# Two attentions of one Trainium2 kernel: where VectorE's copies of transposed rows and the late query tiles stand in the engines' order

## The chip, the cores and the metric

One core of one Trainium2 chip runs one program. The metric is device time in microseconds of one execution; the median of several executions is given. Five engines work beside each other, each through its own list of instructions in order: TensorE (matmuls and transposes, PE in the profile; its weight loads are PEld), VectorE (DVE), ScalarE (ACT), GpSimd (POOL) and SyncE (SP, which issues DMAs). They meet at counting semaphores. All data here is 32-bit.

## The reference, cut to what matters

For 512 tokens of width 1024 a first block (windowed attention, gated convolution, 32 routed experts) is followed by two attention layers, each with an MLP. The two attentions behind the experts are the ones that the change touches:

- layer 0: eight heads of a forgetting attention ("fox": causal softmax with a bias from a running sum) and eight heads of a latent attention over the 256 keys with the best index scores:

```
logits = einsum('bqhd,bshd->bhqs', qb, k) * scale + cq - cum_k     # fox
p = masked_softmax(logits, causal);  o = einsum('bhqs,bshd->bqhd', p, v)
logits = (qa . c_sel + qr . kr_sel) * scale                        # latent
p = masked_softmax(logits, valid);   o = einsum('bqhk,bqkr->bqhr', p, c_sel)
```

- layer 1: sixteen heads with three gated branches, over compressed keys, over selected blocks and over a window:

```
p_c = masked_softmax(s_c, cmp_end <= t);  p_s = masked_softmax(s_s, ...);  p_w = masked_softmax(s_w, ...)
out = gb0 * o_c + gb1 * o_s + gb2 * o_w
```

## The kernel before, in words

Both attentions are software pipelines over items, with an order per engine that is written out by hand. An item is one head and one tile of 128 queries; with query tile t (0 to 3) it is 128 rows by (t+1)*128 keys wide, so 128, 256, 384 or 512 wide.

**Layer 0** has 64 items (`pairs`): for fox and then latent, for four head pairs, for t = 0 to 3, two heads. So items 8m to 8m+7 are one head pair, and their widths are 128, 128, 256, 256, 384, 384, 512, 512. **Layer 1** has 136 items (`nsa`): eight groups of 17 (t = 0, 1, 2, 3 and then 3, 2, 1, 0), each of 16 items (four heads, two branches, two key groups) and one item of compressed scores ("cmp"), 256 wide.

An item goes through these steps, and each engine's loop over i says at which of its steps item k's turn comes:

1. TensorE: scores of item i into a PSUM bank (L1743 and, for fox, L1749; in layer 1 L2389).
2. VectorE: mask and negated maximum of item i in one instruction, from PSUM into one of seven SBUF tiles `scr` (L3935; in layer 1 L4079). Called the maximum below. Before it stands a wait that the tile is free: the transposes of item i-7 have to be done (`wait_ge(p_turned, i - PROBS + 1)`, L3934, and L4069), with PROBS = 7.
3. ScalarE: exponential with row sums (L2433 is the line of its helper).
4. VectorE: reciprocals of two row sums at once (`weigh_pair`, L3923; `weigh_nsa`, L4046, and for a cmp item L4049 to L4052).
5. GpSimd: the product with the reciprocal (L1419; L1443, L1439).
6. TensorE: transposes of item k, at its step i = k + 7, into `psT[k % 2]` (L1765; L2402). There are only these two banks of PSUM for them, so before the transposes of item k it waits until item k-2 has been copied out (`p_copied`, `n_copied`).
7. The copy of the transposed rows into SBUF: even k on ScalarE, odd k on VectorE (L3945; L4087). In VectorE's loop the copy of item k stands at step i = k + 6, behind the maximum of item k + 6 and ahead of that of item k + 7.
8. TensorE: products with the values (L1731; L2352, L2342), at its steps k + 10, once per four items.

In layer 0 TensorE computes the scores of items i and i+1 together at even i. VectorE also takes the low half of finished outputs (L3089, `pair_out_lo`, `nsa_out_lo`), at step k + 13 for the last item k of a head pair.

The waits and the order at the copy in layer 0, on VectorE:

```
if i >= PROBS:
    dve.wait_ge(p_turned, i - PROBS + 1)
nc.vector.tensor_tensor_reduce(out=pair_probs[i % PROBS]..., in0=pair_bank(i)..., accum_out=negm...)
if 2 <= i < n_pairs and i % 2:
    weigh_pair(i)
k = i - TURN_LAG - 1                      # TURN_LAG is 5
dve.wait_ge(p_turned, k + 1); tensor_copy(pair_turned[k % TURNED]..., psT[k % 2]...)
```

**Late query tiles.** In layer 1 four of the eight query tiles (queries 4 to 7) and four sets of compressed scores are made inside the loop, as eight jobs (`NSA_JOBS`) at TensorE's steps `NSA_STEPS`. They use two banks in turn, so a job waits until the job two before it has been taken out. A query tile is taken out by two copies on ScalarE (`queries`, the high parts) and then two subtractions on VectorE (L3089, `nsa_q`). TensorE has filler matmuls that compute nothing needed (L2360) at steps 4 to 15. For i < 16 the scores of layer 1 have two banks, so the scores of item i wait for the maximum of item i-2; later there are four.

The constants at the head of the file: `TURN_LAG, VALUE_LAG = 5, 8`, `PROBS, TURNED = 7, 8`, `AHEAD, MORE_BANKS = 2, 16`.

Of the kernel before, what the change touches and what calls it, by code (L numbers as in the profile page):

```python
# [39 lines left out]
TURN_LAG, VALUE_LAG = 5, 8  # L40
# [114 lines left out]


NSA_JOBS = (("cmp", 0), ("cmp", 1), ("query", 4), ("query", 5), ("query", 6), ("query", 7), ("cmp", 2), ("cmp", 3))
NSA_STEPS = (3, 4, 5, 6, 7, 9, 12, 13)


def nsa_job(what, n):
# [213 lines left out]
def build(nc, w, out):  # L375
    ctx = ExitStack()
    with ctx:
# [307 lines left out]
        for g in range(2):  # L685
            for t in range(NT):
                lo, hi = max(0, t - 1), min(NT - 1, t + 1)
                n = (hi - lo + 1) * P
# [1734 lines left out]
        def _(act):  # L2423
# [11 lines left out]
            def evac(n, o, width=512, f=ACT.Copy, **kw):  # L2435

                product(act, n)
                A(o, bank(n)[:, 0:width], f, **kw).then_inc(proj_evacuated[n % 2], 1)
# [582 lines left out]
            def queries(j):  # L3021

                if j < 4:
                    act.wait_ge(nsa_turned, j + 1)
                    o = early_bank(j)
                else:
                    product(act, nsa_job("query", j))
                    o = bank(nsa_job("query", j))
                A(query(j, 0)[0:HD, :], o[0:HD, :], ACT.Copy)
                A(query(j, 1)[HD:P, :], o[HD:P, :], ACT.Copy).then_inc(stack_hi, 1)  # L3030

            def nsa_attention():

                for i in range(n_nsa + VALUE_LAG + AHEAD + 2):
                    if i in PRESPLIT:
                        if i == PRESPLIT[0]:
                            act.wait_ge(n_scores, n_nsa // 2)
                        first_weights("no0", PRESPLIT.index(i))
                    if i - 1 in NSA_STEPS:
                        what, n = NSA_JOBS[NSA_STEPS.index(i - 1)]  # L3040
                        if what == "query":
                            queries(n)
                        else:
                            evac(nsa_job("cmp", n), cmp_scores[:, n, :])
                    k = i - TURN_LAG - 1
                    if 0 <= k < n_nsa and k % 2 == 0:
                        act.wait_ge(n_turned, k + 1)
                        if k >= TURNED:
                            act.wait_ge(n_values, values_before(k - TURNED))
                        A(turned_probs[k % TURNED][:, 0:nsa[k]["n"]], psT[k % 2][:, 0:nsa[k]["n"]], ACT.Copy)\  # L3050
                            .then_inc(n_copied[k % 2], 1)
                    if i < n_nsa:
                        act.wait_ge(n_masked, i + 1)
                        at = probs[i % PROBS][:, 0:nsa[i]["n"]]
                        if nsa[i]["kind"] == "cmp":
                            A(at, at, ACT.Exp).then_inc(n_probs, 1)
                        else:
                            A(at, at, ACT.Exp, bias=negm[:, n_items + i:n_items + i + 1], scale=-1.0,
                              accum_out=sums[:, n_items + i:n_items + i + 1]).then_inc(n_probs, 1)
                    k = i - VALUE_LAG - AHEAD - 1  # L3060
                    if k in bank_ending:
                        it = nsa[k]
                        act.wait_ge(n_values, values_before(k))
                        A(nsa_out_hi[it["c"]][:, :, it["t"] * P:(it["t"] + 1) * P],
                          psO[it["bank"] % 2][:, :].rearrange("p (j n) -> p j n", j=4), ACT.Copy).then_inc(n_out_hi, 1)
# [13 lines left out]
        def _(dve):  # L3079
# [845 lines left out]
            def pair_attention():  # L3925

                for i in range(n_pairs + VALUE_LAG + AHEAD + 4):
                    if i == n_pairs + 1:
                        weigh_pair(i)
                    if i < n_pairs:  # L3930
                        it, col = pairs[i], n_band + i
                        dve.wait_ge(p_scores, i + 1)
                        if i >= PROBS:
                            dve.wait_ge(p_turned, i - PROBS + 1)  # L3934
                        nc.vector.tensor_tensor_reduce(  # L3935
                            out=pair_probs[i % PROBS][:, 0:it["n"]], in0=pair_bank(i)[:, 0:it["n"]], in1=it["mask"], scale=-1.0,
                            scalar=3e38, op0=ALU.add, op1=ALU.min, accum_out=negm[:, col:col + 1]).then_inc(p_masked, 1)
                    if 2 <= i < n_pairs and i % 2:
                        weigh_pair(i)
                    k = i - TURN_LAG - 1  # L3940
                    if 0 <= k < n_pairs and k % 2:
                        dve.wait_ge(p_turned, k + 1)
                        if k >= TURNED:
                            dve.wait_ge(p_values, batches_before(k - TURNED))
                        nc.vector.tensor_copy(pair_turned[k % TURNED][:, 0:pairs[k]["n"]], psT[k % 2][:, 0:pairs[k]["n"]])\  # L3945
                            .then_inc(p_copied[k % 2], 1)
                    k = i - VALUE_LAG - AHEAD - 3
                    if 0 <= k < n_pairs and k % 8 == 7:
                        chunk = pairs[k]["chunk"]
                        dve.wait_ge(p_out_hi, k // 8 + 1)  # L3950
                        tt(pair_out_lo[:, chunk, :], psO[pairs[k]["bank"] % 2][:, :], hT_hi[:, chunk, :].bitcast(F32), ALU.subtract)\
                            .then_inc(p_out_lo, 1)
# [105 lines left out]
            def nsa_attention():  # L4058

                for i in range(n_nsa + VALUE_LAG + AHEAD + 4):  # L4060
                    if i == 1:
                        compressed_values()
                    elif i - 2 in NSA_STEPS and NSA_JOBS[NSA_STEPS.index(i - 2)][0] == "query":
                        queries(NSA_JOBS[NSA_STEPS.index(i - 2)][1])
                    if i < n_nsa:
                        it = nsa[i]
                        dve.wait_ge(n_scores, i + 1)
                        if i >= PROBS:
                            dve.wait_ge(n_turned, i - PROBS + 1)  # L4069
                        at = probs[i % PROBS][:, 0:it["n"]]  # L4070
                        if it["kind"] == "cmp":
                            s3 = at.rearrange("p (j n) -> p j n", j=8)
                            st = cmpst[:, it["index"], :]
                            link(tt(s3, score_bank(i)[:, 0:256].rearrange("p (j n) -> p j n", j=8),
                                    cmpmask[:, it["t"], :].unsqueeze(1).broadcast_to([P, 8, 32]), ALU.add))
                            link(nc.vector.tensor_reduce(st, s3, X, ALU.max))
                            tt(s3, s3, st.unsqueeze(2).broadcast_to([P, 8, 32]), ALU.subtract).then_inc(n_masked, 1)
                        else:
                            nc.vector.tensor_tensor_reduce(  # L4079
                                out=at, in0=score_bank(i)[:, 0:it["n"]], in1=cmask(it["t"]), scale=-1.0, scalar=3e38,  # L4080
                                op0=ALU.add, op1=ALU.min, accum_out=negm[:, n_items + i:n_items + i + 1]).then_inc(n_masked, 1)
                    k = i - TURN_LAG - 1
                    if 0 <= k < n_nsa and k % 2:
                        dve.wait_ge(n_turned, k + 1)
                        if k >= TURNED:
                            dve.wait_ge(n_values, values_before(k - TURNED))
                        nc.vector.tensor_copy(turned_probs[k % TURNED][:, 0:nsa[k]["n"]], psT[k % 2][:, 0:nsa[k]["n"]])\  # L4087
                            .then_inc(n_copied[k % 2], 1)
                    if 2 <= i < n_nsa + 2 and nsa[i - 2]["g"]:
                        weigh_nsa(i - 2)  # L4090
                    k = i - VALUE_LAG - AHEAD - 3
                    if k in bank_ending:
                        it = nsa[k]
                        span = (slice(None), slice(None), slice(it["t"] * P, (it["t"] + 1) * P))
                        dve.wait_ge(n_out_hi, it["bank"] + 1)
                        tt(nsa_out_lo[it["c"]][span], psO[it["bank"] % 2][:, :].rearrange("p (j n) -> p j n", j=4),
                           nsa_out_hi[it["c"]][span].bitcast(F32), ALU.subtract).then_inc(n_out_lo, 1)
# [34 lines left out]
```

## Time and profile before

| what | value |
|---|---|
| median of 3 runs | 1916.68 us (1914.93 to 1918.02) |
| the profiled execution's own time | 1919.38 us |
| its span in the trace | 1917.6 us |
| busy, share of the span | PE 96%, PEld 76%, DVE 54%, ACT 43%, POOL 31% |
| chain that ended last | PE 86%, DVE 4%, DMA 4%, ACT 3%, issue 2% |
| layer 0's pipeline in the trace | about 808.5 to 887 us |
| layer 1's pipeline in the trace | about 1375 to 1540 us |

The profile shows one execution. Times are microseconds from the span's start. A row of the timeline has start, duration, engine, line, operation, what it writes and reads, how many instructions were merged and, in brackets, how long the engine stood idle before it and what ended that. The duration of a matmul row contains the time until its result is there; the next row can start before it is over.

### The profile page before, as it was taken

The numbers are of one execution on the slowest core, as the hardware profiler recorded it, in microseconds if no ns is written. First come the engines' busy times: TensorE is split into PE (matmuls) and PEld (weight loads), VectorE is DVE, ScalarE is ACT, GpSimd is POOL, SyncE is SP. The second block draws the span as 40 slices with busy tenths as digits, with TensorE's granted clock in tenths as the row PEclk, the third lists the DMA queues.
The fourth block names the chain that finished last, engine by engine and source line by source line (L and its number), as shares of the span: only waits on it lengthen the run. The fifth ranks groups of instructions, "written<-read, shape, count | busy, mean of one in ns | idle before, by whom it ended". The sixth has DMA issues, their size and how long they took to land.

```text
span 1917.6 us, 27389 instructions
## 1 busy us (share of the span) xinstructions
PE 1839.3 (96%) x10554; PEld 1451.5 (76%) x10554; DVE 1027.5 (54%) x2006; ACT 828.2 (43%) x1569; POOL 592.6 (31%) x421
## 2 busy tenths in 40 slices
PE   8999999997888999999999999999999999999998
PEld 7878889842223778767888888889888888888886
DVE  3170442521111869663477676842577725767677
ACT  4123651311111543375554544353377655444543
POOL 4344431011110233356322223233055643232221
PEclk9999999999999999999999999999999999999999
DMA  7223404699999412121132223222203012233321
GB/s 236 98 94 118 140 1 154 251 392 419 420 420 370 167 45 88 46 88 35 54 132 88 88 88 120 98 94 67 45 2 89 2 44 88 88 131 108 113 88 45
DMA packets 86867, 252.06 MB, mean 131 GB/s; under 512 B 12212, under 2 KB 19700, under 8 KB 74448
## 3 DMA queue, kind: packets, MB, share of 16 engines
q1 hardware_dynamic: 81344, 238.79, 33.9%
q0 software_dynamic: 4592, 9.30, 1.3%
q8 instruction: 86, 1.41, 0.3%
q10 hardware_dynamic: 800, 2.20, 0.3%
q14 instruction: 45, 0.37, 0.1%
HBM read 241.89 MB, written 15.73 MB: 134 GB/s over the span
## 4 chain that ended last, share of the span: by engine, by line
PE 86%; DVE 4%; DMA 4%; ACT 3%; issue 2%; POOL 0%; ACTq 0%; DVEq 0%; POOLq 0%
PE psA L1606 42%; PE psS L2054 4%; PE psA L1649 3%; DMA ring<-in_w_down_e 3%; PE psA L2018 2%; PE psO L2352 2%; PE psO L1836 2%; PE psT L1836 2%; PE psS L1836 2%; PE psT L2402 2%; DVE x L3089 2%; DMA big<-in_w_down_e 1%; PE psA L1471 1%; PE psA L1785 1%; PE psS L1649 1%
## 5 line engine op out<-in xcount | busy, mean ns | idle before, releaser
L1290 POOL TENSOR_TENSOR w_slot<-ring,w_slot 128x1024 fp32r<-128x1024 f32 (+1 forms) x81 | 214.0, 2656 | 524.7 <-ACT w_slot L2433 524.4
L1606 PE MATMUL psA<-hT_hi,w_slot 128*128 128x512 f32 x960 | 298.2, 390 | 0.0
L2433 ACT ACTIVATE w_slot<-ring 128x1024 fp32r<-128x1024 f32 (+2 forms) x183 | 196.8, 1086 | 164.4 <-DVE ring L3089 75.0
L1606 PEld LDWEIGHTS psA<-hT_hi,w_slot 128*128 128x128 f32 x960 | 180.4, 188 | 37.3
L1606 PE MATMUL psA<-hT_lo,w_slot 128*128 128x512 f32 x480 | 187.0, 390 | 0.0
L3089 DVE TENSOR_TENSOR w_slot<-ring,w_slot 128x1024 fp32r<-128x1024 f32 x98 | 119.9, 1225 | 115.7 <-ACT w_slot L2433 115.7
L3089 DVE TENSOR_TENSOR x<-psA,x 128x512 f32<-128x512 f32 (+1 forms) x186 | 117.1, 662 | 104.2 <-PE psA L1606 68.8
L1606 PE MATMUL psA<-w_slot,hid_part 128*128 128x512 f32 x672 | 161.4, 390 | 0.0
L2433 ACT ACTIVATE big<-psA 128x512 f32<-128x512 f32 (+6 forms) x134 | 61.7, 482 | 208.7 <-PE psA L1606 126.0
L1606 PEld LDWEIGHTS psA<-w_slot,hid_part 128*128 128x128 f32 x672 | 126.2, 188 | 26.1
L2433 ACT ACTIVATE scr<-scr,stat 128x384 f32<-128x384 f32 (+3 forms) x224 | 123.7, 555 | 19.1 <-DVE stat L4079 9.8
L1290 POOL TENSOR_TENSOR ring_lo<-ring,early_hi 128x1024 fp32r<-128x1024 f32 x34 | 82.6, 2432 | 123.1 <-ACT early_hi L2433 123.1
L1443 POOL TENSOR_SCALAR scr<-scr,stat,big 128x128 f32<-128x128 f32 (+3 forms) x128 | 77.5, 616 | 98.0 <-DVE stat L4046 97.8
L1606 PEld LDWEIGHTS psA<-hT_lo,w_slot 128*128 128x128 f32 x480 | 90.2, 188 | 18.5
L2433 ACT ACTIVATE hid_part<-scr 128x512 fp32r<-128x512 f32 x98 | 59.7, 625 | 98.3 <-DVE scr L3089 98.3
L3089 DVE TENSOR_TENSOR hid_part<-scr,hid_part 128x512 fp32r<-128x512 f32 x98 | 99.1, 1035 | 3.0 <-ACT hid_part L2433 1.8
L2054 PE MATMUL psS<-ring,big 128*64 128x512 f32 x192 | 75.9, 686 | 19.9 <-issue 19.9
L3089 DVE TENSOR_TENSOR big<-psA,small 128x512 f32<-128x512 f32 x32 | 20.6, 685 | 135.1 <-PE psA L1471 135.1
L2433 ACT ACTIVATE big<-psS 128x256 f32<-128x256 f32 (+3 forms) x26 | 8.4, 338 | 187.0 <-PE psS L2054 162.0
L1606 PE MATMUL psA<-hT_lo_early,early_hi 128*128 128x512 f32 x224 | 88.2, 394 | 0.0
L1606 PE MATMUL psA<-w_slot,hT_hi 128*128 128x256 f32 x384 | 71.5, 289 | 1.3 <-DVE big L1147 1.1
L2433 ACT ACTIVATE big<-psT 128x384 f32<-128x384 f32 (+3 forms) x120 | 50.8, 424 | 49.8 <-PE psT L2402 31.3
(557 smaller groups left out, 4450.2 us busy)
## 6 DMA issues: line engine op xcount, KB each, us to landing
ring<-in_mlp_w SPq DMA_DIRECT2D x32, 2048.0 KB, 8.1
ring<-in_w_in SPq DMA_DIRECT2D x8, 2048.0 KB, 8.1
ring<-in_w_gate_e SPq DMA_DIRECT2D x14, 1024.0 KB, 16.3
ring<-in_w_up_e SPq DMA_DIRECT2D x14, 1024.0 KB, 20.7
ring<-in_w_down_e SPq DMA_DIRECT2D x13, 1024.0 KB, 28.3
big<-in_w_down_e SPq DMA_DIRECT2D x12, 1024.0 KB, 26.4
ring<-in_ab_w_in SPq DMA_DIRECT2D x5, 2048.0 KB, 8.6
scr<-in_w_down_e SPq DMA_DIRECT2D x7, 1024.0 KB, 27.0
```

Source lines behind the costliest of these rows:

```text
L1290: nc.gpsimd.tensor_tensor(part(w_lo, c), raw_piece(c), part(w_hi, c).bitcast(F32), ALU.subtract)\
L1443: nc.gpsimd.tensor_scalar(at, at, fac[:, n_items + i:n_items + i + 1], gate3[:, it["t"], it["head"], 1 + it["branch"]:2 + it["branch"]], A ...
L1471: ins = pe.transpose(o[:, c * P:c * P + k], a, ident[0:k, 0:k])
L1606: ins = pe.matmul(o, a, b, start=(at == 1), stop=(at == 3 * len(terms)))
L1649: return pe.matmul(o[:, :], a[:, t * P:(t + 1) * P], b[:, k, :], start=(not h and at == 0), stop=(h == 1 and at == 3 * HALF - 1))
L1836: ins = pe.matmul(KEPT_BANK[q][t][:, :], a[:, k, at], b[:, k, :], start=(not e and k == 0 and a is hi and b is wh), stop=(e == LAST - 1 an ...
L2018: ins = pe.matmul(o[at:at + ROWS, :], ehidT[:, p, k * P + at:k * P + at + ROWS], dn[(2 * b + half) % UNITS][:, k, part * 512:(part + 1) * ...
L2054: ins = pe.matmul(psS[p][at:at + ROWS, :].rearrange("p (h n) -> p h n", h=2), xT[:, p, k, at:at + ROWS], gu[(2 * b + half) % UNITS][:, k], ...
L2352: ins = pe.matmul(o[HD * g:HD * (g + 1), at:at + P], v2[:, b, branch, g, 0:HD], pt[g][:, b * P:(b + 1) * P], start=(it["first"] and not br ...
L2402: ins = pe.transpose(psT[k % 2][:, b * P:(b + 1) * P], probs[k % PROBS][:, b * P:(b + 1) * P], ident)
L2433: return nc.scalar.activation(o, i, f, **kw)
L3089: return nc.vector.tensor_tensor(o, a, b, op)
```

## The change

Three places, in both attentions:

- VectorE's copy of odd item k moves from step k + 6 to step k + 8 in layer 0 and from step k + 6 to step k + 7 in layer 1. In layer 1 `weigh_nsa` is moved ahead of the copy within a step.
- In layer 1, ScalarE takes a late query tile out at TensorE's step of that tile instead of one step later, ahead of its own copy and exponential of that step; VectorE at one step later instead of two.
- Query 6 is made at TensorE's step 8 instead of 7.

```
-NSA_STEPS = (3, 4, 5, 6, 7, 9, 12, 13)
+NSA_STEPS = (3, 4, 5, 6, 8, 9, 12, 13)
...
-                    if i - 1 in NSA_STEPS:
-                        what, n = NSA_JOBS[NSA_STEPS.index(i - 1)]
-                        if what == "query":
-                            queries(n)
-                        else:
-                            evac(nsa_job("cmp", n), cmp_scores[:, n, :])
+                    if i in NSA_STEPS and NSA_JOBS[NSA_STEPS.index(i)][0] == "query":
+                        queries(NSA_JOBS[NSA_STEPS.index(i)][1])
+                    if i - 1 in NSA_STEPS and NSA_JOBS[NSA_STEPS.index(i - 1)][0] == "cmp":
+                        n = NSA_JOBS[NSA_STEPS.index(i - 1)][1]
+                        evac(nsa_job("cmp", n), cmp_scores[:, n, :])
...
@@ VectorE, pair_attention (layer 0)
                     if 2 <= i < n_pairs and i % 2:
                         weigh_pair(i)
-                    k = i - TURN_LAG - 1
+                    k = i - TURN_LAG - 3
                     if 0 <= k < n_pairs and k % 2:
                         dve.wait_ge(p_turned, k + 1)
...
@@ VectorE, nsa_attention (layer 1)
-                    elif i - 2 in NSA_STEPS and NSA_JOBS[NSA_STEPS.index(i - 2)][0] == "query":
-                        queries(NSA_JOBS[NSA_STEPS.index(i - 2)][1])
+                    elif i - 1 in NSA_STEPS and NSA_JOBS[NSA_STEPS.index(i - 1)][0] == "query":
+                        queries(NSA_JOBS[NSA_STEPS.index(i - 1)][1])
...
-                    k = i - TURN_LAG - 1
+                    if 2 <= i < n_nsa + 2 and nsa[i - 2]["g"]:
+                        weigh_nsa(i - 2)
+                    k = i - TURN_LAG - 2
                     if 0 <= k < n_nsa and k % 2:
                         dve.wait_ge(n_turned, k + 1)
                         if k >= TURNED:
                             dve.wait_ge(n_values, values_before(k - TURNED))
                         nc.vector.tensor_copy(turned_probs[k % TURNED]..., psT[k % 2]...)\
                             .then_inc(n_copied[k % 2], 1)
-                    if 2 <= i < n_nsa + 2 and nsa[i - 2]["g"]:
-                        weigh_nsa(i - 2)
```

## Rows read from the trace of the kernel before

**Rows 1.** Layers 0, 1: length, busy PE, PEld, DVE, ACT, POOL, clock, DMA

```profile
808.50:876.00 67.50, 66.05 (x554) 43.52 (x555) 44.21 (x188) 52.85 (x163) 39.81 (x64) 1.00 0.26 95
...
1396.00:1527.00 131.00, 130.10 (x1312) 110.47 (x1304) 101.28 (x396) 98.78 (x309) 80.35 (x125) 1.00 0.13 34
```

**Rows 2.** Waits in 840 to 875: us in total, times, longest

```profile
PEld psT L1765 <- POOL scr L1419: 5.0, 11, 0.5
PE psT L1765 <- DVE big L3945: 1.4, 4, 0.3
```

**Rows 3.** Timeline, layer 0, fox, around the copy of item 15

```profile
831.60 0.69 DVE L3945 COPY big<-psT 128x512 f32<-128x512 f32 x1 [1.22 <-PE psT L1765]
...
832.21 0.68 DVE L3935 CUSTOM_DVE_ANT_0 scr<-psA,const 128x512 f32<-128x512 f32 x1
...
832.43 0.54 PE L1765 MATMUL psT<-const,scr 128*128 128x128 f32 x3
...
833.50 0.27 DVE L3945 COPY big<-psT 128x128 f32<-128x128 f32 x1
```

**Rows 4.** Timeline, layer 0, latent: items 27, 29 and 31

```profile
845.51 0.42 DVE L3945 COPY big<-psT 128x256 f32<-128x256 f32 x1 [1.04 <-PE psT L1765]
...
846.57 0.98 PE L1765 MATMUL psT<-const,scr 128*128 128x128 f32 x7
...
847.16 0.56 DVE L3945 COPY big<-psT 128x384 f32<-128x384 f32 x1 [0.47 <-PE psT L1765]
...
847.63 0.55 DVE L3935 CUSTOM_DVE_ANT_0 scr<-psS,big 128x384 f32<-128x384 f32 x1
...
848.71 0.55 DVE L3935 CUSTOM_DVE_ANT_0 scr<-psS,big 128x384 f32<-128x384 f32 x1
...
849.35 0.77 PE L1765 MATMUL psT<-const,scr 128*128 128x128 f32 x5
...
850.88 0.53 PE L1765 MATMUL psT<-const,scr 128*128 128x128 f32 x3 [0.34 <-DVE big L3945]
```

**Rows 5.** Timeline, layer 1: late query tiles 4 to 7, fillers

```profile
1381.81 1.18 ACT L2433 ACTIVATE nsa_q<-psA 64x512 fp32r<-64x512 f32 x2
...
1383.01 1.39 DVE L3089 TENSOR_TENSOR nsa_q<-psA,nsa_q 64x512 fp32r<-64x512 f32 x2 [0.44 <-ACT nsa_q L2433]
...
1384.46 0.66 PE L1471 MATMUL psA<-const,tok 128*128 128x128 f32 x4 [1.63 <-DVE nsa_q L3089]
...
1388.68 0.66 PE L1471 MATMUL psA<-const,tok 128*128 128x128 f32 x4 [1.86 <-DVE nsa_q L3089]
...
1389.48 0.71 PE L2360 MATMUL psO<-const 128*128 128x160 f32 x4
...
1390.41 1.28 PE L2360 MATMUL psO<-const 128*128 128x160 f32 x4
```

**Rows 6.** Timeline, layer 1: items 25, 59 and 63

```profile
1412.72 0.43 DVE L4087 COPY big<-psT 128x256 f32<-128x256 f32 x1
...
1413.38 0.38 PE L2402 MATMUL psT<-const,scr 128*128 128x128 f32 x2
...
1451.83 0.69 DVE L4087 COPY big<-psT 128x512 f32<-128x512 f32 x1
...
1452.76 0.60 PE L2402 MATMUL psT<-const,scr 128*128 128x128 f32 x4
...
1457.28 0.69 DVE L4087 COPY big<-psT 128x512 f32<-128x512 f32 x1
...
1457.89 0.41 DVE L4049 TENSOR_REDUCE big<-scr 128x8 f32<-128x256 f32 x1
...
1458.46 0.60 PE L2402 MATMUL psT<-const,scr 128*128 128x128 f32 x4
...
1458.72 0.68 DVE L4079 CUSTOM_DVE_ANT_0 scr<-psA,const 128x512 f32<-128x512 f32 x1
```

**Rows 7.** Waits in 1385 to 1535: us in total, times, longest

```profile
PEld psT L2402 <- POOL scr L1443: 2.1, 9, 0.3
```

## The prediction, made before the changed kernel ran

> **What bounds the kernel now.** I read the busy times by stretch first, then the chain, the waits of both stretches and the timeline around VectorE's copies. In both attentions TensorE is as good as full: 66.05 of 67.50 us in layer 0 and 130.10 of 131.00 in layer 1 behind its start, at the full clock, while VectorE is busy for 44.21 and 101.28 [rows 1]. Only the start of layer 1 has real holes: TensorE waits 1.63 and 1.86 us for VectorE to take late query tiles out [rows 5]. So whatever makes TensorE wait inside a pipeline is added to the time nearly whole, and what merely makes VectorE's work earlier gains little. TensorE's list is in order, and its transposes of item k+2 cannot start before item k is copied out of the same bank. The question is therefore how much room there is between the end of a copy and those transposes.
>
> **Layer 0: the copy goes behind two maxima.** Item 15 is the last of a head pair and 512 wide. Its copy starts at 831.60 and ends at 832.29; the transposes of item 17 start at 832.43 [rows 3], 0.14 later, which is what the semaphore takes: no room at all. In the latent half the row says so itself, the transposes waited 0.34 us for the copy [rows 4]. Why does the room vanish there? Between the two transposes TensorE has only items 128 wide to do. Now the copy goes behind the maxima of items k+7 and k+8 and a reciprocal. By the wait in the code the maximum of item k+7 can't start before the transposes of item k are done, which is the very thing that the copy waits for. So the maxima don't fill a hole ahead of the copy; they take its place. From the first of the two maxima to what follows the reciprocal it is 832.21 to 833.50, 1.29 us [rows 3]. The copy is later by 1.29, and so are TensorE's next transposes. There are seven such places (items 7, 15, ... 55; after item 63 no maxima are left): 7 x 1.29 = **9.0 us**.
>
> VectorE starts its next instruction before the last one's recorded end: 1.29 holds two maxima of 0.68 and a reciprocal. The Trainium skill, "VectorE: DVE Perf Modes", section "The DRAIN you can't avoid", says that the next operation does not start until the pipe is empty; if one adds whole durations for that, a delay would be at least 1.36 instead of 1.29 and the seven would give 9.5. The start-to-start times of the rows decide, and by them the recorded ends overlap.
>
> The other odd items have room. In the latent half the 256-wide copy (item 27) ends at 845.93 and the transposes that need it start at 846.57 [rows 4]: 0.50 beyond the 0.14. Two 256-wide maxima and a reciprocal take some 0.76 (an estimate, from the 0.42 of a 256-wide copy with some 0.08 of overlap each): 0.26 too late, four times, 1.0 us. The 384-wide one (item 29) ends at 847.72, its transposes' successors start at 849.35 [rows 4]: 1.49 of room; a maximum and the low half of an output (847.63 to 848.71, 1.08) and a second maximum (0.55) make 1.63: 0.14 too late, four times, 0.5 us. In the fox half TensorE has the bias products in between, and both fit. The 128-wide copies have the value products in between. Layer 0 in sum: 9.0 + 1.0 + 0.5 = **+10.6 us** with the rounding. Bounds: the seven alone at half size (maxima partly done ahead of time, which the wait in the code speaks against), +4.5; all of it, +11.
>
> **Layer 1: the copy goes behind one maximum.** The same two waits stand there. Read item by item, the 67 odd items fall in two halves: for about half the value products stand between the two transposes, and the copy has over 0.6 us of room. For 33 they don't. Item 59: copy from 1451.83, end 1452.52, successors at 1452.76 [rows 6], room 0.10; a 512-wide maximum costs 0.69 with its last part: 0.59 too late. Item 25: copy ends 1413.15, successors at 1413.38 [rows 6], room 0.09; a 384-wide maximum costs 0.55: 0.46 too late. Done so for all 26 places of this kind, they range from 0.2 to 0.6 and give 0.39 in mean: 10.1 us. At seven places, once per group of 17, the copy also falls behind the reciprocals of a cmp item, 1457.89 to 1458.72, 0.83 us [rows 6]: item 63's copy would start about 1458.7 instead of 1457.28, and its successors 1.1 us late; 7 x 1.1 = 7.8. All added, 17.9 us. That is the upper end, since TensorE standing still in one place gives VectorE time to catch up before the next, and where VectorE is behind anyway two such delays aren't paid twice. The lower end is half, 9. I take **+13.5**, the middle: TensorE is full here [rows 1], which argues for the upper end, VectorE is busy 77% of this stretch, which argues for less.
>
> **The start of layer 1: late query tiles earlier.** Query 4 is transposed before 1381. ScalarE takes it out from 1381.81 in 1.18 us, VectorE from 1383.01 in 1.39, and query 6 starts at 1384.46, after 1.63 of waiting; query 7 at 1388.68, after 1.86 [rows 5]. In the changed order ScalarE starts on query 4 a step earlier, about 1380.9, so VectorE is done about 1383.5; and query 6 comes a step later, at about 1384.1. Its wait goes. Query 5 follows on both engines: done about 1385.8, when TensorE has reached query 7. That wait goes too: 3.5 us. What is late next: query 6 is taken out by ScalarE only behind its exponential of item 7, until 1388.0, and by VectorE until 1389.4; behind that stands the maximum of item 9, on which the scores of item 11 wait (two banks). TensorE is there at about 1388.0 and waits until 1389.8. And query 7 holds the maximum of item 10 until 1391.9. Followed on to the transposes of item 5 (step 12), TensorE is there at 1392.4, 2.3 us earlier than now, and I take **-2.0**. Best case: both waits go and so does the stretch at half clock behind them (below), -4.1; worst case 0, if ScalarE's earlier tile makes exponentials late.
>
> **Reciprocals earlier.** In layer 1 they no longer stand behind a copy. GpSimd gets its work earlier, and TensorE's waits for GpSimd are 2.1 us in sum [rows 7]; half of that, **-1.0**; bounds 0 and -2.1. In layer 0 the same row has 5.0 us in 11 waits [rows 2], but they are the weight loads' idle time, while the matmuls waited for VectorE alone 1.4; I give it nothing, at most -1.5.
>
> **Sum.** +10.6 + 13.5 - 2.0 - 1.0 = +21.1 us. The profiled execution took 1919.38 in all (span 1917.6); with the change 1940.5. The median of the runs is 2.7 lower, so the median with the change is **1938 us**.
>
> **Rivals.**
>
> *The copies are harmless, the softmax chain is what counts: faster.* If the maxima, once ahead of the copies, let exponentials, reciprocals and GpSimd run ahead so far that TensorE's transposes stop waiting for GpSimd, and if the room behind a copy is larger than I read, the change gains: 2.0 to 4.1 at the start, up to 2.1 in layer 1 [rows 7] and up to 1.5 in layer 0. About 1911. It decides from the point at which the transposes of item k+2 start less than 0.1 us later than now. Against it stands that they start 0.14 us behind the copy's end now [rows 3], and that the maxima can't start earlier than the transposes allow. Chance 0.12.
>
> *Only layer 0's delays are real.* VectorE in layer 1 is often behind, so one maximum more or less ahead of a copy may vanish in its backlog, and reciprocals come earlier. Then +10.6 - 3.0 and some 2 of layer 1: about 1926. Chance 0.2.
>
> *The waits also cost clock.* After the waits for query tiles TensorE fell from 2.4 to 1.2 GHz for a while: four fillers took 1.28 instead of 0.71 us [rows 5]. A wait of 1.3 us in each head pair is nearly as long as those. If each of the seven brings such a stretch, at about 1.7 us each (an estimate: half of a stretch like that one, in which the scores, transposes and fillers between 1390.2 and 1393.6 took twice their time), it adds up to 12: 1950. The Trainium skill, "TensorE: Matmul & The Clock Gate", section "A second HAM failure mode: psum-queue depth-cycling", describes a kernel whose TensorE idles shortly between groups while it cycles through banks and whose clock swings for it. By that rule this case would come; against it, the 1.63 us wait before query 6 was not followed by it. Chance 0.13.
>
> *Nothing much happens* (delays of one sort make up for gains of the other within 0.2%): chance 0.03, at 1917.
>
> **Numbers.** My own case has 0.52 and about 1931 to 1946. Measurements of this kernel can tell 0.2% from nothing, 3.8 us. Faster 0.12, same 0.04, slower 0.84. The range leaves out the faster case and the farthest of the clock case: 1922 to 1952.
>
> **What would show it.** Right: in the timeline the 512-wide copy of layer 0 starts 1.3 us behind the end of its transposes, after two maxima and a reciprocal; the next transposes carry a wait of 1.3 to 1.5 us for `big` L3945, seven times; a head pair takes 1.3 us longer in fox and 1.7 longer in latent. In layer 1 TensorE waits for `big` L4087 some 30 times for 0.3 to 1.1 us. The queries' transposes at about 1384.1 and 1386 (plus what layer 0 has added) carry no long wait. Wrong: the maxima start ahead of the transposes of item k, the head pair keeps its length, or the gap between the copy's end and the next transposes grows beyond 0.14.

## The result, and the profile after

The changed kernel took 1947.94 us in the median of four runs (1947.32 to 1949.2), the kernel before 1917.35 beside it: ratio 1.0163 [1.0145, 1.018], slower by 31 us. The prediction was 1938, slower by 21. The sign and the mechanism were right and the range of 1922 to 1952 held the time; the sum was 10 us short, and the time lies 2 us above the 1931 to 1946 of the prediction's own case, on the side of the rival with the clock (1950). The profiled execution took 1947.32, its span of 1945.5 is 27.9 longer than before's.

The page's head, and busy times by stretch as in [rows 1] (length, then busy PE, PEld, DVE, ACT, POOL, clock, DMA share, GB/s; the first stretch, 725 to 900, holds the last of the experts' work and layer 0's pipeline, the other two lie inside the pipelines):

```profile
span 1945.5 us, 27389 instructions
...
PE 1843.3 (95%) x10554; PEld 1448.5 (74%) x10554; DVE 1024.6 (53%) x2006; ACT 831.0 (43%) x1569; POOL 592.4 (30%) x421
...
725.00:900.00 175.00, 160.62 (x1079) 122.63 (x1078) 113.85 (x354) 82.04 (x213) 74.83 (x83) 0.98 0.17 61
...
806.00:890.00 84.00, 70.70 (x557) 46.17 (x557) 45.99 (x193) 54.60 (x168) 40.55 (x65) 0.96 0.21 76
...
1407.00:1555.00 148.00, 131.68 (x1301) 108.94 (x1297) 103.04 (x394) 101.13 (x310) 79.72 (x125) 1.00 0.11 30
```

The stretch with the same work before the change:

```profile
727.00:887.00 160.00, 157.28 (x1080) 120.86 (x1080) 113.45 (x353) 82.33 (x213) 75.23 (x84) 1.00 0.19 67
```

Read the rows of 725 to 900 and of 727 to 887 together. The same work (1079 and 1080 matmul entries) took 175 instead of 160 us. TensorE's idle time in it went from 2.7 to 14.4 us, and its busy time from 157.28 to 160.62, at a granted clock of 0.98 instead of 1.00. So layer 0 holds two different losses: 11.7 us of waiting and 3.3 of slower clock. VectorE did the same work, 113.85 and 113.45. In layer 1's pipeline TensorE stands still for 16.3 of 148 us, where it stood for 0.9 of 131 [rows 1]. No engine became the bound; the engines wait in turn.

The waits of layer 0's stretch 805 to 900, then those of 1387 to 1565 (engine, what it wanted to write and its line, what it waited for; us in total, times, longest):

```profile
DVE scr L3934 <- PE psT L1765: 34.3, 27, 4.0
...
PE psT L1765 <- DVE big L3944: 12.8, 15, 1.7
...
PEld psT L1765 <- POOL scr L1419: 1.0, 3, 0.3
```

```profile
DVE scr L4078 <- PE psT L2402: 44.4, 55, 2.8
...
PE psT L2402 <- DVE big L4088: 14.4, 29, 1.2
...
PEld psT L2402 <- POOL scr L1443: 5.7, 8, 1.4
```

For VectorE's copies TensorE waited 1.4 us in 840 to 875 before [rows 2], and not once in layer 1. Now they cost it 12.8 us in layer 0 and 14.4 in layer 1. The first line of each fence is the other half: the maxima (`scr` L3934, L4078) are now what stands first behind a transposition, 27 and 55 times. In layer 0 it was the copies before, and it is one copy now (before in 805 to 890, then the changed kernel in 805 to 900):

```profile
DVE big L3945 <- PE psT L1765: 25.8, 24, 2.6
```

```profile
DVE big L3944 <- PE psT L1765: 3.9, 1, 3.9
```

The maxima did not fill a hole ahead of the copy; they took its place.

Item 15's surroundings in the timeline of the changed kernel (start, duration, engine and line; in brackets how long it waited and for whom), to be laid beside [rows 3]:

```profile
831.62 0.69 DVE L3934 CUSTOM_DVE_ANT_0 scr<-psA,const 128x512 f32<-128x512 f32 x1 [1.22 <-PE psT L1765]
...
832.24 0.69 DVE L3934 CUSTOM_DVE_ANT_0 scr<-psA,const 128x512 f32<-128x512 f32 x1
...
832.85 0.16 DVE L3922 RECIPROCAL stat<-stat 128x2 f32<-128x2 f32 x1
...
832.93 0.67 DVE L3944 COPY big<-psT 128x512 f32<-128x512 f32 x1
...
833.75 0.53 PE L1765 MATMUL psT<-const,scr 128*128 128x128 f32 x3 [1.37 <-DVE big L3944]
```

The maximum starts at 831.62, where the copy stood at 831.60 before. (That the two traces meet here is chance: the changed one came into the layer 1.8 us earlier and had lost as much in the first head pair.) The copy starts at 832.93, 1.31 behind that maximum, and its successors 0.15 behind its end, at 833.75 instead of 832.43. Seven such waits stand in the layer: 1.37 us ahead of items 9 and 17, 1.74 ahead of items 25, 33, 41 and 49 (where 0.34 had been before), and 1.23 ahead of item 57. The same in layer 1, item 63, to be laid beside [rows 6]:

```profile
1475.46 0.41 DVE L4048 TENSOR_REDUCE big<-scr 128x8 f32<-128x256 f32 x1
...
1476.29 0.68 DVE L4078 CUSTOM_DVE_ANT_0 scr<-psA,const 128x512 f32<-128x512 f32 x1
...
1476.90 0.69 DVE L4088 COPY big<-psT 128x512 f32<-128x512 f32 x1
...
1477.73 0.63 PE L2402 MATMUL psT<-const,scr 128*128 128x128 f32 x4 [0.77 <-DVE big L4088]
```

Head pair by head pair (transposes of item 8m+1 to those of item 8m+9, the timeline's start times) layer 0 took, in us:

```
pair         1     2     3      4     5     6      7    sum
before     8.25  9.86  9.82   8.62  8.63  8.64   8.63  62.45
after      9.99 11.20 12.83  10.66 10.57 12.14  10.57  77.96
```

Each pair is 1.3 to 2.0 longer, the latent ones (4 to 7) more than the second and third of fox; two of them, the third and the sixth, carry another 1.6 at half clock.

### The profile page after: what moved, and what is told of

It reads as the page before. It is cut to its first block, busy times and chain, and to the rows that moved or that the text cites. A ratio compares the mean times of both kernels' runs of the same rounds, so it can differ in the third digit from the quotient of the medians.

```text
span 1945.5 us, 27389 instructions
## 1 busy us (share of the span) xinstructions
PE 1843.3 (95%) x10554; PEld 1448.5 (74%) x10554; DVE 1024.6 (53%) x2006; ACT 831.0 (43%) x1569; POOL 592.4 (30%) x421
## 3 DMA queue, kind: packets, MB, share of 16 engines
q8 instruction: 86, 1.41, 0.3%
## 4 chain that ended last, share of the span: by engine, by line
PE 82%; DVE 7%; DMA 5%; issue 3%; ACT 2%; POOL 1%; DVEq 0%; SPq 0%; ACTq 0%; POOLq 0%
PE psA L1606 42%; PE psS L2054 4%; PE psA L1649 3%; DMA ring<-in_w_down_e 3%; PE psA L2018 2%; PE psO L2352 2%; PE psO L1836 2%; PE psT L1836 2%; PE psS L1836 2%; PE psT L2402 2%; DMA big<-in_w_down_e 2%; DVE x L3088 1%; PE psA L1471 1%; PE psA L1785 1%; PE psS L1649 1%
## 5 line engine op out<-in xcount | busy, mean ns | idle before, releaser
L2402 PE MATMUL psT<-const,scr 128*128 128x128 f32 x336 | 60.3, 277 | 16.1 <-DVE big L4088 14.4
```

The costliest lines, as they stand in the source:

```text
L2402: ins = pe.transpose(psT[k % 2][:, b * P:(b + 1) * P], probs[k % PROBS][:, b * P:(b + 1) * P], ident)
```

## The experiments

The theory on record: a copy has as much room as stands between its end and the transposes that reuse its bank; what it is moved beyond that is added whole. The rivals: the lost time comes from the query tiles or the reciprocals; the waits cost clock; room does not matter. Each kernel was timed against the kernel before on the same chip (before's medians 1916.8 to 1917.6); a difference in us is the ratio less 1, times 1917. All compute the whole of the reference.

**e1: only layer 0's copies.**

```
-                    k = i - TURN_LAG - 1
+                    k = i - TURN_LAG - 3
```

> The kernel before with the layer 0 part of the change alone: VectorE's copy two steps later. Theory (the copy is late, and the next transposes wait for it in one of two banks): in the trace of the change layer 0 took 15.6 us more, so +15 to +16 us, some 12.5 us of it waits of the transposes for `big` on VectorE in 15 places and about 3 us from two stretches at 1.2 GHz. Rival (the loss comes from the two parts together, or from the experts ahead, which moved by 1.8 us between the two traces): under +8 us.

Measured: 1931.69, ratio 1.0074 [1.0057, 1.0091], +14.2 us. Its waits in 805 to 900:

```profile
PE psT L1765 <- DVE big L3945: 12.7, 15, 1.7
```

That is the changed kernel's row, almost to the digit. In the trace the layer is 15.5 us longer in both, so layer 0's loss is the copy's alone.

**e2: only layer 1's copies and reciprocals.**

```
-                    k = i - TURN_LAG - 1
+                    if 2 <= i < n_nsa + 2 and nsa[i - 2]["g"]:
+                        weigh_nsa(i - 2)
+                    k = i - TURN_LAG - 2
...
-                    if 2 <= i < n_nsa + 2 and nsa[i - 2]["g"]:
-                        weigh_nsa(i - 2)
```

> The kernel before with the layer 1 order of VectorE alone: reciprocals ahead of the copy, copy one step later; late query tiles as before. Theory: every place where no value products stand between the transposes of items k and k+2 pays one maximum, +18 us by the trace of the change (from item 3 to item 135 the distance between the two traces grew from -2.6 to +15.6 us), less at the start, where the fillers leave room: +17 to +19. Rival (VectorE was behind anyway and the maximum is lost in its backlog): +8 to +12, and the rest of the difference would come from the query tiles.

Measured: 1935.68, 1.0101 [1.0084, 1.0119], +19.4 us, more than the 13.5 - 1.0 of the sum. Its interval, 16.1 to 22.8 us, leaves room for the sum's upper end of 17.9. In the trace it falls back by 18.2 us from item 9 to item 134. Waits in 1384 to 1550:

```profile
PE psT L2402 <- DVE big L4089: 14.4, 29, 1.2
```

e1 and e2 together make +33.6; with e3's -1.3 (below) that is +32.3 against the +31.2 of the whole. The parts add up within their intervals.

**e3: only the query tiles, with query 6 at step 8.** `NSA_STEPS` and both engines' `queries` as in the change, the rest as before.

> The kernel before with the late query tiles alone taken earlier (and query 6 at step 8); both copies where they were. Theory: the transposes of item 5 come 2.6 us earlier, as in the trace of the change, and nothing behind takes it back: -2 to -3 us. Rival (the earlier start runs into the softmax chain of the 128- and 256-wide items, where ScalarE and VectorE are nearly full, and is given back by item 20): 0 to -1.

Measured: 1915.71, 0.9993 [0.9985, 1.0002], -1.3 us. Its late query tiles, beside [rows 5]:

```profile
1381.90 0.65 PE L1471 MATMUL psA<-const,tok 128*128 128x128 f32 x4 [1.14 <-ACT big L2433]
...
1384.01 0.60 PE L1471 MATMUL psA<-const,tok 128*128 128x128 f32 x4
...
1385.30 0.62 PE L1471 MATMUL psA<-const,tok 128*128 128x128 f32 x4
...
1388.96 0.44 PE L2389 MATMUL psS<-nsa_k,nsa_q 128*128 128x128 f32 x2 [1.33 <-DVE stat L4078]
```

Queries 6 and 7 (second and third row) wait no more, as predicted: 3.5 us of waiting gone. In its place stand 1.14 us of query 5 waiting for ScalarE, which the sum did not have, and 1.33 of item 11's scores behind VectorE's maximum of item 9, which it had. Counted from the entry into layer 1, e3 runs 2.5 us ahead of before from item 5 to the end of the layer.

**e4: e3 with the reciprocals ahead of the copies, which keep their step.**

```
+                    if 2 <= i < n_nsa + 2 and nsa[i - 2]["g"]:
+                        weigh_nsa(i - 2)
                     k = i - TURN_LAG - 1
...
-                    if 2 <= i < n_nsa + 2 and nsa[i - 2]["g"]:
-                        weigh_nsa(i - 2)
```

> The same, and the reciprocals of layer 1 ahead of the copy within a step, the copy itself at its old step. Theory: a reciprocal of two columns ahead of the copy costs the copy 0.08 us in half of the places, but once per group of 17 the reciprocals of a compressed item (0.83 us) come ahead of a copy that has 0.1 to 0.4 us of room: some 0.5 us at up to seven places, so +1 to +4 us against the run with the query tiles alone. Rival (earlier reciprocals feed GpSimd sooner, and that counts): 1 us faster than the run with the query tiles alone.

Measured: 1916.07, 0.9996 [0.9988, 1.0005]. No gain over e3; the times alone do not tell the two apart. In the trace the transposes of items 5 to 134 take 0.9 us longer than e3's (141.2 and 140.3). It is lost in steps at items 31 (0.75), 65 (0.3) and 99 (0.7), where the reciprocals of a cmp item stand ahead of a copy, and 0.7 of it comes back by item 116. Waits in 1384 to 1530:

```profile
PE psT L2402 <- DVE big L4088: 1.2, 2, 0.6
```

**e5: layer 0 as in the change, but items 7, 15, ... 63 copied at the old step.**

```
-                    k = i - TURN_LAG - 1
-                    if 0 <= k < n_pairs and k % 2:
+                    for k in (i - TURN_LAG - 3, i - TURN_LAG - 1):
+                        last = k == i - TURN_LAG - 1
+                        if 0 <= k < n_pairs and k % 2 and (k % 8 == 7) == last:
...
```

> Layer 0 as in the change, layer 1 as before, but in layer 0 the last odd copy of each head pair (items 7, 15, ... 63, 512 wide) stands at its old step; the other 24 odd copies stay two steps later. Theory (TensorE pays where a copy has no room): the seven waits of 1.4 us go, and with them the two stretches at 1.2 GHz, since no long wait is left; what stays are items with little room: 0.2 to 0.4 us at four latent places each of 256 and 384 wide: +1.5 to +3.5 us against the kernel before, instead of +15. Rival (any later copy costs, by what is queued behind it): about three quarters of the loss stays, +11.

Measured: 1919.1, 1.0012 [1.0002, 1.0021], +2.3 us. One copy in four put back takes away 11.9 of e1's 14.2 us. Its waits in 805 to 890:

```profile
PE psT L1765 <- DVE big L3946: 3.5, 13, 0.3
```

What is left, some 0.54 us per latent head pair, is that of the 256- and 384-wide copies (0.40 in the prediction). Their waits are 0.29 and 0.16 us, where the prediction had 0.26 and 0.14.

**e6: layer 0's copies one step later instead of two.** `k = i - TURN_LAG - 2`.

> Layer 0 alone, all odd copies one step later instead of two: behind one maximum. Theory (each maximum ahead of a copy without room costs its own length, 0.61 to 0.75 us): seven places x 0.75 = 5.2 us, the others have room; no stretch at 1.2 GHz, as the waits are too short: +4.5 to +6. If the clock takes part already: +7 to +8. Rival (a fixed price for a copy that isn't taken at once): as much as with two maxima, +15.

Measured: 1923.12, 1.0035 [1.0022, 1.0049], +6.7 us, less than half of what two steps cost. Waits in 805 to 890, and a 512-wide copy's surroundings in the timeline:

```profile
PE psT L1765 <- DVE big L3945: 6.2, 7, 1.1
```

```profile
853.01 0.69 DVE L3935 CUSTOM_DVE_ANT_0 scr<-psA,big 128x512 f32<-128x512 f32 x1 [0.70 <-PE psT L1765]
...
853.62 0.69 DVE L3945 COPY big<-psT 128x512 f32<-128x512 f32 x1
...
854.46 0.53 PE L1765 MATMUL psT<-const,scr 128*128 128x128 f32 x3 [1.06 <-DVE big L3945]
```

Now only one maximum, 0.61 from start to start, stands ahead of the copy, and each head pair is 0.72 longer. The size follows the number of maxima, and the other copies have room for one.

**e7 and e8: layer 1's odd copies parted by their room.** Both start from e3. The copy of an odd item is made one step later if value products stand behind its transposes (e7, 31 copies, the diff below), or if none do (e8, 34 copies, from item 11 on; its last line is `return k > 7 and not any(values)`); the rest are copied at the old step. The two differ in one more thing: in e8 the reciprocals stand ahead of every copy, as in the change, in e7 only ahead of those that are made later. e4 prices that at 0.9 us.

```
+            def copied_later(k):
+
+                values = [j in range(n_nsa) and nsa[j]["closes"] and nsa[j].get("j") != 3 for j in (k - 3, k - 2)]
+                return any(values)
...
+                    nsa_copy(i - TURN_LAG - 1, False)
                     if 2 <= i < n_nsa + 2 and nsa[i - 2]["g"]:
                         weigh_nsa(i - 2)
+                    nsa_copy(i - TURN_LAG - 2, True)
```

> The late query tiles as in the change; in layer 1 only those 31 odd copies go one step later behind whose transposes TensorE has value products to do before the next odd transposes; the other 37 stay at the old step, reciprocals where they were. Theory: these copies have over 0.6 us of room and the later order costs nothing: within 0.5 us of the run with the query tiles alone, in the trace and timed. Rival (a later copy also delays what stands behind it on VectorE): +3 us or more against that run.

> The complement: query tiles and reciprocals as in the change, and in layer 1 only the copies without value products behind them go one step later (items 11, 15, 17 and so on, 34 of them); the 31 with room and items 1 to 7 stay. Theory: these places carry the whole loss of layer 1, 18 us by the trace of the change from item 3 to the end: +15 to +17 against the kernel before (with the 2.5 us that the query tiles give). Rival (the loss is spread over all places): half, +7.

Measured: e7 1916.05, 0.9999 [0.999, 1.0008]; e8 1933.11, 1.0092 [1.0077, 1.0108], +17.6 us. The waits in 1384 to 1550, of e7 and then of e8:

```profile
PE psT L2402 <- DVE big L4064: 1.3, 4, 0.5
```

```profile
PE psT L2402 <- DVE big L4064: 14.7, 29, 1.3
```

Of two halves that move nearly as many copies by the same step, one costs nothing that the times can show and the other the whole of the loss. This shows the room rule most plainly. "Nothing" is not quite true in the trace: e7's layer 1 is 1.1 us longer than e3's (0.4 by item 12, 0.7 to 0.9 from item 29 on, 1.1 at the end), more than the 0.5 that was expected at most. The row says where: TensorE waits ahead of items 11, 15, 29 and 127 (0.23, 0.31, 0.20 and 0.54 us), each time for one of the later copies. So value products behind the transposes are a good sign of room and no proof of it; four of the 31 copies had too little.

**e9: the room made larger instead, on TensorE's side.** If room is what counts, value products put between the transposes of a 512-wide item and those that reuse its bank help the order of before. e3, and in layer 0 the value products of items 8m+3 two steps later:

```
                     k = i - VALUE_LAG - AHEAD
+                    if k % 8 in (3, 5):
+                        k -= 2
                     if 0 <= k < n_pairs and k % 4 == 3:
```

> The copies at their old steps, the query tiles earlier, and in layer 0 the value products of the first four items of a head pair (0.8 us) moved on TensorE from step k + 10 to step k + 12, so that they stand between the transposes of the last odd item and the next odd ones: room made where there is none. Theory (room between the transposes is what counts): the 0.34 us waits of the latent half, some 0.2 us of it real, go: 1 us less in layer 0, -2 us against the kernel before together with the query tiles. Rival (ScalarE's copies, which wait for these products, hold up exponentials): layer 0 longer by 1 us or more.

Measured: 1913.36, 0.9977 [0.9968, 0.9986]: faster than both kernels, by 4.4 us against before (interval 2.7 to 6.1), 3 of them beyond e3, more than the 2 that were expected. In the trace a latent head pair takes 8.28 us instead of 8.63, and layer 0 is 1.5 us shorter, so half of the gain over e3 is seen there:

```profile
845.10 0.77 PE L1765 MATMUL psT<-const,scr 128*128 128x128 f32 x5
...
845.80 0.88 PE L1731 MATMUL psO<-big 128*64 128x128 f32 x12
...
845.81 0.67 DVE L3946 COPY big<-psT 128x512 f32<-128x512 f32 x1
...
847.03 0.59 PE L1765 MATMUL psT<-const,scr 128*128 128x128 f32 x3
```

The 512-wide copy now runs beside twelve value products (0.88 us), and the transposes behind it carry no wait, where they had 0.34 [rows 4]. The other half of the gain is not shown to be the products'. Nine of e9's eleven executions have a mean granted clock of 0.990 or more, but only nine of the 21 of before beside them. Among executions at 0.990 alone the medians are 1913.4 (eight) and 1914.9 (nine), 1.5 us apart.

**e10: the same room under the late copies.** e1 with e9's products.

> Layer 0 with VectorE's copies two steps later (+14.9 us), and the same value products moved into the gap; query tiles as before. Theory: the products fill 0.8 us of each of the seven waits of 1.4 us, and the waits that are left are too short for a stretch at 1.2 GHz: 5.7 us and 3 us less, so +6 to +9 against the kernel before. Rival (what the transposes wait for is not the copy's end but something behind the maxima): still +13 or more.

Measured: 1926.13, 1.0046 [1.0031, 1.0062], +8.8 us, 5.4 less than e1. The latent head pairs, however, did not get shorter: 10.56 us as in e1. Its waits in 805 to 890 and the places around item 8m+7:

```profile
PE psT L1765 <- DVE big L3947: 10.8, 17, 1.0
```

```profile
852.83 0.74 PE L1765 MATMUL psT<-const,scr 128*128 128x128 f32 x5 [0.97 <-DVE big L3947]
853.50 0.88 PE L1731 MATMUL psO<-big 128*64 128x128 f32 x12
...
854.91 0.67 DVE L3947 COPY big<-psT 128x512 f32<-128x512 f32 x1
...
855.73 0.53 PE L1765 MATMUL psT<-const,scr 128*128 128x128 f32 x3 [0.93 <-DVE big L3947]
```

The products gave the 512-wide copy room and took it from the one before, whose successors now wait 0.97. With the maxima ahead, three of four odd transpositions of this half wait for a copy, and the copies stand behind maxima. That looks like a closed loop through two engines, whose length does not depend on where TensorE does its other work; the equal 10.56 us of e1 and e10 fit it, and nothing else was tried. What e10 gained in the trace lies elsewhere: 1.5 us in the first three pairs, and 3.2 because its profiled execution had none of the half-clock stretches that e1's had in this layer. So the time came out where it was expected (+6 to +9), but not by the expected account, in which the products were to save 5.7 us.

**e11: the query tiles earlier, but query 6 left at step 7.** `NSA_STEPS` as before.

> The query tiles earlier on ScalarE and VectorE as in the change, but query 6 left at TensorE's step 7; copies as before. Theory (query 6 at step 8 is part of the gain, since at step 7 its bank is not free yet): TensorE waits 0.6 us or so at step 7, and ScalarE then takes query 6 out ahead of the exponential of item 7: within 1 us of the run with query 6 at step 8. Rival (the step is what made the gain): 1.5 us or more slower than that run.

Measured: 1915.45, 0.9992 [0.9983, 1.0001]. Counted from the entry into layer 1, its trace is 2.5 us ahead of before from item 5 on, just as e3's. Query 6 carries no wait at step 7 either (its transposes start at 1384.01, behind 1.14 us of query 5 waiting for ScalarE). Neither the traces nor the times show anything that hangs on step 8.

## Why the prediction was right, and where it was short

**The mechanism.** That the maxima take the copy's place instead of filling a hole ahead of it was read from a wait in the code and from a gap of 0.14 in [rows 3]. The changed kernel shows both, and e5, e7 and e8 show the converse: copies with room can be moved for next to nothing, those without cost the whole distance. The rival in which the copies are harmless fell with this, and so did "only layer 0's delays are real": e2 and e8 cost as much in layer 1 as e1 in layer 0.

**Layer 0, seven 512-wide copies, 9.0 us.** Predicted 1.29 each; the copy starts 1.31 behind the maximum, and the fox pairs two and three are 1.35 to 1.41 longer (the changed kernel and e1, where no half-clock stretch falls in). What was missed is small and occurs in every pair: the copy used to start 0.04 behind the end of its transposes and the maximum starts 0.15 behind them, so the chain grows by 0.1. The prediction had set against its rows what one gets by adding whole durations, at least 1.36, from the Trainium skill, "VectorE: DVE Perf Modes", section "The DRAIN you can't avoid". That number lies close, but the trace does not bear out its reason: the two maxima start 0.62 apart at a recorded 0.69 (831.62 and 832.24 above), so their recorded times overlap as the rows of before had it.

**Layer 0, the 256- and 384-wide ones, 1.0 + 0.5.** e5 gives 0.54 per latent head pair instead of 0.40. With the first pair's 1.74, where 1.29 was expected, layer 0 without its half-clock stretches is 12.3 us longer, where the sum had 10.6, and more than the 11 that it called its upper bound.

**The clock, not in the sum.** The other 3.2 us of layer 0 are two stretches at half clock. One of them, with what stands ahead of it and behind:

```profile
830.00:834.70 4.70, 3.33 (x27) 2.32 (x27) 2.89 (x12) 2.80 (x9) 2.40 (x4) 1.00 0.01 2
834.70:838.10 3.40, 3.40 (x28) 2.45 (x24) 0.29 (x4) 0.76 (x5) 1.52 (x2) 0.50 0.02 5
838.10:842.00 3.90, 3.90 (x34) 2.85 (x32) 2.12 (x9) 2.57 (x8) 0.88 (x2) 1.00 0.00 0
```

TensorE had just waited 1.37 us for item 15's copy; it then worked without a break for 3.40 us at 0.50 of the clock, 1.2 GHz, and went on at 2.4. The price, 1.6 us each, is what the rival said (1.7). But of seven such waits two were followed by one, not seven: in the changed kernel those ahead of items 17 and 41, in e1, with the same code in this layer, those ahead of items 25 and 49. The Trainium skill, "TensorE: Matmul & The Clock Gate", section "A second HAM failure mode: psum-queue depth-cycling", tells of a kernel that cycles through banks and whose TensorE idles shortly between groups often enough for the clock to swing; this trace agrees in kind, for two waits out of seven. No other profiled execution has such a stretch in layer 0, those of e6 and e10 among them, with waits of up to 1.07 and 0.97 us. That speaks for the long waits as the cause and does not show it. The rival was true in part, worth 3 of its 12 us.

**Layer 1's delays, 13.5.** This is the step that failed. From item 3 to item 135 the changed kernel falls back by 18.2 us against before. All places added had given 17.9. These places were right: the seven places with cmp reciprocals take 7.9 us together, where it had 7.8, and the others 10.3, where it had 10.1. The prediction then took "the middle" because VectorE is behind in places anyway and catches up while TensorE stands still. The runs show no such discount. A full TensorE gives nothing back between two places, and VectorE's backlog only matters if it was there before the change: each place was costed from the room the trace shows, in which the backlog is already counted. The haircut of 4.4 us had no row under it.

**Reciprocals ahead of the copies, -1.0.** Wrong in sign. e4 against e3 shows a loss of 0.9 us in the trace, and no gain in the times. GpSimd's row, on which the gain rested [rows 7], was idle time of the weight loads, like the one that the prediction had rightly set aside in layer 0; and the cmp reciprocals are 0.83 us ahead of a copy [rows 6].

**Query tiles, -2.0.** Timed -1.3 (interval -2.9 to +0.4), in the trace -2.5. The trace flatters it: before's profiled execution has a half-clock stretch that e5's lacks, with the same code in layer 1. First before, the stretch and what stands ahead of it, then e5:

```profile
1385.00:1390.20 5.20, 3.34 (x30) 3.10 (x28) 3.54 (x10) 3.92 (x12) 0.87 (x2) 1.00 0.00 0
1390.20:1393.60 3.40, 3.40 (x18) 2.91 (x21) 2.22 (x9) 2.36 (x9) 0.88 (x2) 0.51 0.00 0
```

```profile
1384.00:1389.00 5.00, 2.55 (x20) 2.12 (x18) 2.44 (x7) 2.48 (x8) 0.86 (x2) 1.00 0.00 0
1389.00:1394.00 5.00, 3.96 (x33) 3.13 (x33) 3.70 (x13) 3.78 (x12) 0.90 (x3) 1.00 0.00 0
```

From item 5 on before is 1.6 us behind e5 for that alone. So about 1 us of e3's 2.5 comes from where the tiles stand. The rest is not all chance either: the stretch stands in three of six profiled executions with the tiles' old place (before, e1, e6, not e2, e5, e10) and in none of seven with the new one.

**The sum again**, in the trace: 12.3 (layer 0 at full clock) + 3.2 (clock) + 18.2 (layer 1's places, which hold the cmp reciprocals) - 2.5 (query tiles) = +31.2. Against +21.1 that is 1.7 in layer 0's sizes, 3.2 in the clock, 4.7 in layer 1's delays (4.4 of it the discount), 1.0 in the gain from reciprocals that did not come, less 0.5 in the query tiles: 10.1. The spans differ by 27.9 only. 1.8 us of the rest is that the experts ahead of layer 0 were done earlier in the changed kernel's profiled execution (their last stretch starts at 724.58 instead of 726.38), and 1.5 came between the layers, where before has a half-clock stretch at 1322 and the changed kernel none. Both are in stages that the change does not touch.

**Open.** What decides whether a wait is followed by half clock. Where the half of e9's gain comes from that its trace does not show in layer 0. And whether the maxima would fill the hole ahead of the copy if they did not have to wait for the transposes, with one more `scr` tile: that was not tried.

## What to carry to other kernels

Before moving an instruction behind others in an in-order queue, look at what they wait for: if it is the same event as its own, they fill no hole but take its place, and the move costs the whole time from the start of the first to the start of the moved one wherever that had no room. Room is read from the trace as the time from its end to the start of the work that reuses its bank, less the hand-over; sum it place by place, and where the waiting engine is full take the sum whole, without a discount. Room is better made than spent: with other work of TensorE put behind the tightest copies layer 0 became 1.5 us shorter in the trace, with the copies in the order of before. But look at where that work comes from: under the late copies (e10) the same move only shifted the wait to the copy before.

## What the runs showed of the chip that was not expected

The same code has a half-clock stretch of 3.4 us in one execution and none in another: at about 1320 in seven of thirteen profiled executions (before, e3, e4, e5, e7, e8, e11), at about 1390 in three, in layer 0 two in the changed kernel and two in e1. Each costs 1.4 to 1.6 us where two executions of the same code could be laid side by side, more than the 1 us or so that the query tiles' new place is worth. The spread of the timed executions goes with the clock: of the 21 of the kernel before beside e9, the nine with a mean granted clock of 0.990 took 1913.5 to 1916.2 us and the nine with 0.988 took 1917.9 to 1919.9. A difference of under 2 us between two single traces of this kernel is therefore no finding before both have been looked through for them.

A 512-wide maximum of VectorE that waits for the end of the transposes started 0.15 us behind it, the copy in its place 0.04. That is small, but paid once in each round of the loop through TensorE and VectorE.
